# Rows 8 to 15 of the down product as a third group of seven products, with sums of rows kept in HBM meanwhile

## The reference

```python
def swiglu(x, w_gate, w_up, w_down):
    return (jax.nn.silu(x @ w_gate) * (x @ w_up)) @ w_down

x = x + 0.5 * rmsnorm(swiglu(h, w1_gate[i], w1_up[i], w1_down[i]), g_ffn1_post[i])
```

## Time and profile before

| | us |
|---|---|
| median of 3 runs (lowest to highest) | 2745.42 (2745.37 to 2745.59) |
| profiled execution, own time | 2745.79 |
| its span, first to last instruction | 2744.0 |
| TensorE busy | 2734.4 |
| VectorE, ScalarE, GpSimd busy | 1967.3, 1583.9, 133.4 |
| DMA moved | 353.64 MB, mean 129 GB/s |

### The profile page before, as it was taken

One profiled execution on the slowest core, in us unless ns is written; L12 is line 12 of the kernel. 1 busy time (PEld: TensorE's weight loads), 2 busy tenths in 40 slices (PEclk: granted clock), 3 DMA queues, 4 the chain that ended last, 5 costly groups with the idle time before them and its releaser, 6 DMA issues.

```text
span 2744.0 us, 45038 instructions
## 1 busy us (share of the span) xinstructions
PE 2734.4 (100%) x18186; PEld 2477.3 (90%) x18186; DVE 1967.3 (72%) x2659; ACT 1583.9 (58%) x2464; POOL 133.4 (5%) x150
## 2 busy tenths in 40 slices
PE   9999999999999999999999999999999999999999
PEld 8999987599999899999976799999987889999988
DVE  7768666767676587776657587685876746988858
ACT  6556543665565585565526565565754546666645
POOL 0000000000000000000000000000001100000000
PEclk9999999999999999999999999999999999999999
DMA  7775414037764227774231247754233223776531
GB/s 217 179 185 150 131 55 102 16 100 185 190 179 124 85 85 204 175 190 120 72 90 53 93 130 178 188 135 131 77 96 93 90 79 101 179 194 173 146 131 54
DMA packets 156414, 353.64 MB, mean 129 GB/s; under 512 B 34736, under 2 KB 58672, under 8 KB 156208
## 3 DMA queue, kind: packets, MB, share of 16 engines
q1 hardware_dynamic: 139936, 292.03, 34.3%
q0 software_dynamic: 16128, 58.73, 12.6%
q10 hardware_dynamic: 144, 0.00, 0.0%
HBM read 346.52 MB, written 2.10 MB: 127 GB/s over the span
## 4 chain that ended last, share of the span: by engine, by line
PE 99%; DVE 1%; ACT 0%; DMA 0%; issue 0%; SPq 0%; DVEq 0%; ACTq 0%
PE banks L716 31%; PE banks L718 31%; PE banks L717 31%; PE banks L1266 1%; PE banks L1288 1%; PE banks L1325 1%; PE banks L1277 1%; PE banks L1329 0%; PE banks L1315 0%; PE banks L755 0%; PE banks L1419 0%; DVE PT L3056 0%; PE banks L1248 0%; DMA X<-in_x 0%; PE banks L1212 0%; PE banks L1161 0%
## 5 line engine op out<-in xcount | busy, mean ns | idle before, releaser
L716 PE MATMUL banks<-HH,WH 128*128 128x256 f32 (+1 forms) x3084 | 970.4, 315 | 0.8 <-DVE HL L2239 0.7
L717 PE MATMUL banks<-HH,WL 128*128 128x256 f32 (+1 forms) x3084 | 965.6, 313 | 0.0
L718 PE MATMUL banks<-HL,WH 128*128 128x256 f32 (+1 forms) x3084 | 965.3, 313 | 0.0
L716 PEld LDWEIGHTS banks<-HH,WH 128*128 128x128 f32 x3084 | 588.3, 191 | 43.5 <-issue 8.0
L717 PEld LDWEIGHTS banks<-HH,WL 128*128 128x128 f32 x3084 | 588.4, 191 | 34.8 <-issue 1.0
L718 PEld LDWEIGHTS banks<-HL,WH 128*128 128x128 f32 x3084 | 588.4, 191 | 34.1
L591 DVE TENSOR_TENSOR WL<-raw,WH 128x1024 fp32r<-128x1024 f32 (+2 forms) x300 | 362.0, 1209 | 241.9 <-ACT WH L586 241.1
L586 ACT ACTIVATE WH<-raw 128x1024 fp32r<-128x1024 f32 (+2 forms) x300 | 310.9, 1039 | 269.4 <-PE banks L718 145.1
L718 PE MATMUL banks<-SL,WH 128*128 128x256 f32 x1472 | 416.6, 283 | 0.0
L716 PE MATMUL banks<-SH,WH 128*128 128x256 f32 x1472 | 416.6, 283 | 0.0
L717 PE MATMUL banks<-SH,WL 128*128 128x256 f32 x1472 | 416.6, 283 | 0.0
(11 more groups left out here) (335 smaller groups left out, 3572.0 us busy)
## 6 DMA issues: line engine op xcount, KB each, us to landing
extra_raw<-in_w_quarters SPq DMA_DIRECT2D x96, 512.0 KB, 4.2
raw<-in_w_quarters SPq DMA_DIRECT2D x54, 512.0 KB, 4.5
raw<-in_w_in SPq DMA_DIRECT2D x46, 512.0 KB, 3.7
raw<-in_w_down SPq DMA_DIRECT2D x45, 512.0 KB, 3.7
extra_raw<-in_w_quarters POOLq DMA_DIRECT2D x36, 512.0 KB, 6.8
spare_raw<-in_w_quarters SPq DMA_DIRECT2D x30, 512.0 KB, 4.3
extra_raw<-in_last_quarters SPq DMA_DIRECT2D x26, 512.0 KB, 4.2
raw<-in_w_quarters POOLq DMA_DIRECT2D x24, 512.0 KB, 6.2
```

Of the source, the lines that this page charges most:

```text
L716: e.matmul(o, wh, ah, start=start, stop=False, skip_group_check=skip)
L717: e.matmul(o, wl, ah, start=False, stop=False, skip_group_check=skip)
L718: return e.matmul(o, wh, al, start=False, stop=stop, skip_group_check=skip)
```

## The change

The late rows are now a third down group of seven products, g = n + 2, with the operands of hidden rows 8 to 15. It needs four sums of these rows (`late_sum` 0 to 3). Their place in SBUF, `HLF` and a new view `HHF` on the same area, is wanted for the first two groups' sums. So VectorE makes the late sums early, under groups 9 and 10, GpSimd stores each to a scratch in HBM (`gpsimd_park`, 512 KB), and brings them back into `HLF` under the second down group (`gpsimd_fetch`). Which half of the down matrix comes first is turned round, and the layout of the host's quarters now holds rows 0 to 15. The results of the groups are gathered in a different way (`vector_half_add`, seeds that ScalarE copies to the banks of the last rows).

The core of the diff:

```diff
-        self.half_rows(s, "early", down, l, down_half(early))
-        for g in seven_groups(s)[-2:]:
+        for g in seven_groups(s)[-3:]:
             for ph in range(PHASES):
                 self.add((s, "seven", g, ph))
-        self.half_rows(s, "late", down, l, 1 - down_half(early))
...
+        HHF = at("HHF", [P, DC, T], F32, halves_at)
...
+            if i == 0:
+                e.wait_ge(*parked[3].at(s))
             e.activation(row_sums(HH, i), row_sums(HLF, i), ACT.Copy).then_inc(*act.done(("row_sum_high", s, i)))
...
             if i == 0:
-                e.wait_ge(*vec.at("hidden", s, DOWN_SEVEN - 1))
-                e.wait_ge(*pe.at("gate_up1", s, 3))
+                e.wait_ge(*parked[2].at(s))
...
+        def vector_late_sum(e, s, i):
+
+            def rows(t, j):
+                return HIDF[:, DOWN_SEVEN + j:DOWN_WHOLE:2, part(t)]
+            a, b = row_sums(HLF, 0), row_sums(HHF, 0)
+            out, one, other, op = ((a, rows(1, 0), rows(1, 1), ALU.subtract), (b, a, rows(0, 0), ALU.subtract),
+                                   (a, rows(0, 0), rows(1, 0), ALU.subtract), (b, rows(0, 1), b, ALU.add))[i]
...
+            if i > 1:
+                e.wait_ge(*parked[i - 2].at(s))
+            e.tensor_tensor(out, one, other, op).then_inc(*vec.done(("late_sum", s, i)))
...
+                if g == 9:
+                    vector_late_sum(e, s, 1)
                 vector_weight_sum(e, s, g, 6)
                 split_low(e, W[s, "seven", g, 6])
                 split_low(e, after_seven(s, g, 0))
+                if g == 9:
+                    vector_late_sum(e, s, 2)
                 if g == n - 1:
                     vector_hidden_low(e, s, 8)
                     vector_hidden_low(e, s, 9)
-                    vector_row_sum(e, s, 2)
...
                 vector_half_scale(e, s, g, 0)
+                if g == n - 1:
+                    vector_hidden_low(e, s, 10)
+                    vector_hidden_low(e, s, 11)
                 split_low(e, after_seven(s, g, 2))
                 if not conv:
                     vector_half_hidden(e, s, g, 0)
+                if g == 8:
+                    vector_late_sum(e, s, 0)
+                if g == 9:
+                    vector_late_sum(e, s, 3)
                 if g == n - 2:
                     vector_row_sum(e, s, 0)
+                if s == 0 and g in (5, 7):
+                    vector_tables(e, g == 7)
             vector_early_rows(e, s)
             vector_first_down_seven(e, s, n)
             vector_second_down_seven(e, s, n + 1)
-            for i, u in enumerate([W[s, "late", 3]] + [W[s, "down", k] for k in range(DOWN_WHOLE, 2 * n)]):
-                split_low(e, u)
...
+            vector_third_down_seven(e, s, n + 2)
...
             if s > 8:
                 vector_conv_half(e, s, n - 1, 0)
-            vector_hidden_low(e, s, 10)
-            vector_hidden_low(e, s, 11)
...
+                    if g == seven_groups(s)[-1]:
+                        for i in (0, 1) if q == "sum" else (2, 3):
+                            gpsimd_fetch(e, s, i)
+                if g == 9:
+                    gpsimd_park(e, s, 0)
+                if g == 10:
+                    for i in (1, 2, 3):
+                        gpsimd_park(e, s, i)
+
+        def gpsimd_park(e, s, i):
+
+            e.wait_ge(*vec.at("late_sum", s, i))
+            e.dma_start(sums[i].rearrange("p (k t) -> p k t", k=4), row_sums(HHF if i % 2 else HLF, 0)).then_inc(
+                *parked[i].done((s,)))
+
+        def gpsimd_fetch(e, s, i):
+
+            e.wait_ge(*parked[i].at(s))
+            e.wait_ge(*pe.at("seven", s, gated_groups(s) + 1, SUM_PRODUCTS[i]))
+            e.dma_start(row_sums(HLF, i), sums[i].rearrange("p (k t) -> p k t", k=4)).then_inc(*fetched[i].done((s,)))
```

More of the change, by code:

```diff
@@ L440, in build_program @@
         added = {q: sem(f"s_weights_added_{q}", 16) for q in ADDED}
+        parked = [sem(f"s_sums_parked{i}", 16) for i in range(4)]
+        fetched = [sem(f"s_sums_fetched{i}", 16) for i in range(4)]
         params_in = sem("s_params", 16)
@@ L451, in build_program @@
         stored = sem("s_stored", 16)
+        sums = nc.dram_tensor("parked_sums", (4, P, UNIT), F32, kind="Internal").ap()
         W = Weights(a)
@@ L561, in tiles_free @@
             if s is not None and STAGES[s] == "ffn":
[L562 to L565, removed]
+                e.wait_ge(*pe.at("unit", W[s, "seven", seven_groups(s)[-1 - (tile_of[u] == NSPLIT + 1)], 6]))
             elif s is not None and STAGES[s] == "mix":
@@ L1024, in tensor_ffn @@
                 tensor_seven(e, s, g)
[L1025 to L1026 removed]
+            tensor_early_rows(e, s)
+            for g in seven_groups(s)[-3:]:
                 tensor_seven(e, s, g)
[L1028 removed]
             added = [[vec.at("quarter_added", s, t, m) for t in range(2)] for m in range(2)]
+            early, late = (list(range(4 * half, 4 * half + 4)) for half in (n_groups % 2, 1 - n_groups % 2))
             tensor_last_rows(e, s, [W[s, "down", k] for k in range(DOWN_WHOLE, 2 * n_groups)],
@@ L1049, in tensor_half_rows @@
                         last = trio(e, ps[4 * half + i][:], high_of(u)[:, c], low_of(u)[:, c], HIDH_HIGH[:, k, :],
-                                    HIDL_LOW[:, k, :], opens and kp == j == 0, opens and kp == 3 and j == 1, not opens)
-                last.then_inc(*pe.done((name, s, kp), ("unit", u)))
+                                    HIDL_LOW[:, k, :], kp == j == 0, kp == 3 and j == 1)
+                last.then_inc(*pe.done(("early", s, kp), ("unit", u)))
         def token_high(s):
@@ L1644, in after_seven @@
                 return W[s, "early", i]
-            return W[s, "seven", g + 1, i] if g <= gated_groups(s) else W[s, "late", i]
+            return W[s, "seven", g + 1, i] if g < seven_groups(s)[-1] else W[s, "down", DOWN_WHOLE + i]
         def scalar_full(e, s, *chunks):
@@ L1887, in scalar_tokens, with scalar_late_sum_high @@
+            scalar_hidden_high(e, s, DOWN_WHOLE)
+            scalar_hidden_high(e, s, DOWN_WHOLE + 1)
+            for i in (2, 3, 0, 1):
+                scalar_seed(e, s, i)
+        def scalar_late_sum_high(e, s, i):
+            e.wait_ge(*fetched[i].at(s))
+            e.activation(row_sums(HH, i), row_sums(HLF, i), ACT.Copy).then_inc(*act.done(("late_sum_high", s, i)))
         def scalar_tokens(e, s, tokens):
@@ L1889, in scalar_tokens @@
             if s == LAST:
-                e.wait_ge(*pe.at("unit", W[s - 1, "late", 3]))
+                e.wait_ge(*pe.at("unit", W[s - 1, "seven", seven_groups(s - 1)[-1], 6]))
             e.activation(token_high(s)[:], tokens[:], ACT.Copy).then_inc(*act.done(("tokens_high", s)))
@@ L2646, in vector_ffn @@
             vector_second_down_seven(e, s, n + 1)
-            for i, u in enumerate([W[s, "late", 3]] + [W[s, "down", k] for k in range(DOWN_WHOLE, 2 * n)]):
-                split_low(e, u)
-                for k in range(DOWN_WHOLE + 2 * i, min(DOWN_WHOLE + 2 * i + 2, 2 * n)):
-                    vector_hidden_low(e, s, k)
-                if s == 0 and i == 0:
-                    vector_tables(e)
-                if conv and u == W[s, "down", 20]:
+            vector_third_down_seven(e, s, n + 2)
+            for k in range(DOWN_WHOLE + 2, 2 * n):
+                for row in range(2 * k - DOWN_WHOLE - 2, min(2 * k - DOWN_WHOLE, 2 * n)):
+                    vector_hidden_low(e, s, row)
+                split_low(e, W[s, "down", k])
+                if conv and k == 20:
                     vector_tokens(e, LAST, PTOK2)
@@ L3383, in build_program @@
             program(counting)
-        for signal in (*landed, *added.values(), high, low, pe, act, vec, pool, params_in, gains_in, consts_in, *first_gate_in, *x_in, x_second_in, pos_in, tokens_in, rope_in,
+        for signal in (*landed, *added.values(), *parked, *fetched, high, low, pe, act, vec, pool, params_in, gains_in, consts_in, *first_gate_in, *x_in, x_second_in, pos_in, tokens_in, rope_in,
                        small_in, stored):
```

238 lines of the change are left out of this document (146 added, 92 removed).

## The result

The changed kernel takes 2782.8 us (median of 4 runs, 2781.6 to 2783.5), the kernel before 2745.5 in the same series: ratio 1.0136 (95% interval 1.0118 to 1.0153). It is slower by 37 us, where 12.6 were forecast, and lies 17 us above the range. The profiled execution took 2783.3, its span is 2781.5.

The account below looks back on a forecast made before the run. TensorE's instruction stream was taken as the bound. 2745.8 - 8.2 - 0.9 + 5.3 + 12.8 + 3.6 = 2758.4, as a median 2758.0 us; own range 2751 to 2764, 8-in-10 range 2740 to 2766.

Parts of the forecast that it names:

- gain A: Third group of five FFN stages: 168 matmuls of 256 columns replace 96 of 512, saving 1.64 us a stage, 8.2 in all.
- rival D: Third group or stage's end waits on later fetches or loads, 1.5 us a stage over the forecast: 2765.5 us; 9%.
- gain B: Last FFN stage: splitting rows 10 and 11 earlier shortens the 1.31 us wait on low parts, gain 0.9 us (0 to 1.31).
- loss C: Stage 0: sine and cosine tables ahead of two half scales delay product 3 by 3.2 and 2.1 us, 5.3 in all.
- lead of 1.9 us: Usual group: ScalarE's copy ends at 115.07 and product 3 starts at 116.97, so shorter delays of the copy are covered.
- product 3: Product of a group, counted from 0, whose bank ScalarE must first copy out; lead 1.9 us usually, 0.76 in last gated group.
- product 5: Last FFN stage, group 10: where TensorE was to meet the late half scale, lead 1.9 us, cost 3.6 us.
- loss E: Last gated group: late sum 3 and row sum 0 wait for stores; 3.2 us in each of four stages, 12.8 in all.
- 1.55 a store: GpSimd's queue behind group 10's third weight addition: each store adds 1.55 us, the middle taken; store 1 lands 216.45, store 2 218.0.
- rival C: TensorE's clock falls to its lower level after idle stretches, about 1.5 us lost at each of seven: 2768 us; 6%.
- Rivals A and B: A: stores land in time, 2743.8 us, 23%. B: VectorE's idle time takes everything up, whole gain, 2736.3 us, 12%.

Follow-up runs that it names:

- the queue's repair: The changed kernel with stores 1 to 3 issued by SyncE instead of GpSimd, against the kernel before: 2749.2 us (ratio 1.0015).

## Why the prediction was wrong, point by point

**The stream (gain A)** was right: 20.16 us against 21.79 in four stages. In the fifth the third group takes 22.95 with the waits inside it (below, rival D). **The wait of the last stage (gain B)** went altogether, 1.3 where 0.9 was taken.

**The tables (loss C)** were right in place and size: waits of 3.16 and 2.10, forecast 3.2 and 2.1. The lead of 1.9 us read from one copy and one matmul held to 0.1 us.

**The products were miscounted in words.** What the prediction calls product 3 and product 5, counted from 0, are products 2 and 4: 217.77 is 5.77 us, two products, behind the group's start at 212.00. The rows and leads are those of the right instructions, so no number hangs on it, save in the last stage: there TensorE met the delay at product 3, whose weight split stands behind the late sum (2554.24 on VectorE, 2555.51 on TensorE), a product earlier than forecast. The size, 3.40 for 3.6, came out in part by luck: the split was 4.7 us late with a lead of 1.3, where 5.5 less 1.9 had been worked out.

**The stores (loss E) were mis-sized**: 12.8 us forecast in four stages, 22.7 measured. In stage 0 the addition goes out 1.9 us later relative to its group (3.3 us ahead of the group's start at 219.46, before 5.2 ahead of 212.00) where 1.1 had been worked out, and landed 6.7 us on (7.0 taken). Store 1 landed 1.3 us behind it (1.55 taken), 0.3 us later than forecast. The step that failed is "1.55 a store" for store 2: the bound reckoned transfers that follow each other in a queue, but the issue itself was held back, so store 2 paid its whole way alone, 224.53 to 227.9, and landed 3.7 us behind store 1, in each of the four stages. Its own way is 3.3 us. The prediction's estimate by the Trainium skill (the page "DMA: Bandwidth & Descriptors", section "Anatomy of one DMA — SWDGE (gpsimd) path") is 3.2 us for such a transfer, and for store 2 the trace agrees with it. For store 1, which went out right behind the addition, it does not: 7.4 us. Rows of before could not show the hold: all transfers of GpSimd there have 128 pieces. But the diff and the order did show `512x1x256` in place of `128x1024`, and nothing was made of it; of two unlike kinds of transfer one should not have bounded the other.

**The clock (rival C)** was given 6% and taken as an alternative, at 1.5 us for each of seven waits. It came with the forecast's waits, not instead of them: seven times, 1.5 to 2.7 us, 13.1 in all. The argument against it was the granted clock after one wait of 1.31 us, while the forecast itself reckoned waits of 3 us. What follows from the forecast's own waits belongs into its sum. The Trainium skill ("TensorE: Matmul & The Clock Gate", Part 1) says that idleness brings the lower level; the trace agrees behind seven of the eight waits. That rule should have weighed more than the one short wait.

**Rival D** was in part true as well: in the last FFN stage the fourth fetch went out at 2660.39, only when the third had landed, 9.7 us behind it, and its sum reached TensorE 2.37 us late. It is the same hold of GpSimd's queue, whose timeline in the changed kernel reads:

```profile
2650.70 0.96 POOL L3439 DMA_DIRECT2D HLF<-parked_sums  x1
2660.39 0.75 POOL L3439 DMA_DIRECT2D HLF<-parked_sums  x1 [8.72 <-issue]
```

In the stages 0 to 6 the fetches follow each other in the same way and TensorE does not wait for them. Of the profiled executions this one alone has a wait of over 1 us there.

**Rivals A and B** were wrong for this kernel, but A's number (2743.8) is what the queue's repair comes near to: 2749.2. Of the 5.4 us between, the slow stretches of the tables are 3.0, and group 10 costs 3.9 in the five stages where A took 2.2.

Of the 24.8 us between forecast and result, 9.9 are the waits for the stores in four stages (8.6 of them the hold, 3.7 us in place of 1.55 four times), 13.1 the clock and 2.4 the late fetch, with -0.6 in the rest. So two steps failed, and each alone would have put the time above the range of 2740 to 2766: store 2 at 1.55 us, and the slow matmuls behind the forecast's own waits, which stood in the sum at nothing. The store and the fetch arose from one fact that stood in the order; the clock was a rival that should have been a term.

## What to carry to other kernels

Where TensorE never waits, the first thing to read is the lead at the tightest place in each helper's order, not its idle share; a block longer than the lead belongs in single steps, and an instruction that waits for a DMA behind everything on which TensorE depends next. Every idle stretch of 2 us or more in the forecast is to be priced with the slow matmuls behind it (35 of 40 here, 1.4 to 2.7 us each). Before a DMA is put into GpSimd's queue its pieces are to be counted, and it is to be asked what stands behind it there.

## What the runs showed of the hardware

- GpSimd holds back the issue of a transfer of 512 pieces of 1 KB while another such is under way (6.7 and 2.9 us of "issue"), not that of one of 128 pieces of 4 KB behind a transfer of the same kind. Behind an addition of 128 pieces a store of 512 goes out at once. A held transfer went out 0.30 to 0.36 us after the landing of the one ahead, in 24 places. VectorE stood idle for 2.68 of these 6.72 us, so it is not VectorE's work that holds GpSimd there. SyncE issued a store of 512 pieces 0.1 to 1.0 us before the one ahead had landed, in five places of the three runs that store from it, so it does not hold back to the landing; a longer overlap was not tried there, nor how many pieces fit.
- TensorE's clock and waits: the profiles of the changed kernel and of the experiments hold 46 waits of over 1.2 us between matmuls of 256 columns. Behind the 6 of at most 1.85 us the matmuls ran at the full clock. Of the 40 of 2.09 us and more, 35 had a slow stretch behind them, at a price of 1.4 to 2.7 us, and 5 had none (2.10, 2.14, 2.37, 2.94 and 3.16 us long). Waits of 2.10 and 3.16 us at the same place of other kernels had one. So between 2.1 and 3.2 us the length of a wait does not decide it; what does is left open.
